# The z projection, its gate and norm inside the state-space units, and the late modulation inside the merge

## The reference, cut to what matters

```
y = y_ssd * silu(z)                                  # z = h @ w_z, 512 x 1024
yg = y in 4 groups of 256 columns
yg = yg * rsqrt(mean(yg * yg) + EPS)
ys = (yg * g_ssd_norm) @ w_branch_ssd
ya = o_attn @ w_branch_attn
mix = (sigmoid(g_a) * ya + sigmoid(g_s) * ys) @ w_out
```

## Time and profile before

| | us |
|---|---|
| median of 3 runs | 3477.12 (3476.56 to 3481.98) |
| the profiled execution | 3473.39 |
| its span | 3471.7 |
| PE busy in the span | 3009.3 (87%) |
| VectorE busy | 1838.7 (53%) |
| ScalarE busy | 1370.1 (39%) |
| GpSimd busy | 469.2 (14%) |
| mean granted clock | 0.933 |

### The profile page before, as it was taken

How to read it: one execution, slowest core, us unless ns; L and a number is a source line. 1 busy time by engine, 2 the same in 40 slices (tenths; PEclk the granted TensorE clock), 3 DMA queues, 4 the chain that set the end, 5 groups by cost and what they waited for, 6 DMA issues and landing times. The chain is left out here.

```text
span 3471.7 us, 37403 instructions
## 1 busy us (share of the span) xinstructions
PE 3009.3 (87%) x14782; PEld 2431.3 (70%) x14782; DVE 1838.7 (53%) x2198; ACT 1370.1 (39%) x1810; POOL 469.2 (14%) x524
## 2 busy tenths in 40 slices
PE   7976679798698679999999359979999897889998
PEld 4854568687487548777777248668888796668887
DVE  4456663535332448888888453644543415545543
ACT  3311222516222328788787122333332323433332
POOL 0006102212000052223222100000000004100000
PEclk9988889999799689999999779989999998999999
DMA  5200450200431339999998640043322202033321
GB/s 185 55 0 1 163 183 1 62 12 1 133 89 45 110 141 360 359 362 369 379 374 325 276 133 21 29 82 97 107 89 96 73 26 82 25 62 97 97 97 49
DMA packets 319998, 455.61 MB, mean 131 GB/s; under 512 B 69552, under 2 KB 251440, under 8 KB 298704
## 3 DMA queue, kind: packets, MB, share of 16 engines
q1 hardware_dynamic: 299136, 419.40, 35.4%
q0 software_dynamic: 20688, 33.82, 2.7%
HBM read 450.77 MB, written 39.08 MB: 141 GB/s over the span
## 5 line engine op out<-in xcount | busy, mean ns | idle before, releaser
L274 PE MATMUL banks<-hT_r,weight_part 128*128 128x512 f32 x1056 | 428.2, 405 | 72.9 <-DVE weight_part L234 58.4
L234 DVE TENSOR_TENSOR weight_part<-weights,weight_part 128x2048 fp32r<-128x2048 f32 (+1 forms) x118 | 264.3, 2240 | 417.6 <-ACT weight_part L223 417.6
L279 PE MATMUL banks<-hT_r,weight_part 128*128 128x512 f32 x1056 | 418.2, 396 | 0.0
L223 ACT ACTIVATE weight_part<-weights 128x2048 fp32r<-128x2048 f32 (+1 forms) x118 | 218.8, 1854 | 346.3 <-PE banks L274 279.2
L278 PE MATMUL banks<-h_low,weight_part 128*128 128x512 f32 x864 | 337.8, 391 | 0.0
L274 PEld LDWEIGHTS banks<-hT_r,weight_part 128*128 128x128 f32 x1056 | 201.8, 191 | 120.9 <-DVE weight_part L234 59.9
L279 PEld LDWEIGHTS banks<-hT_r,weight_part 128*128 128x128 f32 x1056 | 200.8, 190 | 47.9
L278 PEld LDWEIGHTS banks<-h_low,weight_part 128*128 128x128 f32 x864 | 163.8, 190 | 37.7 <-issue 2.4
L1136 ACT ACTIVATE up_room<-banks,conv_bias,taps 128x512 f32<-128x512 f32 x88 | 68.1, 777 | 297.4 <-PE banks L279 297.4
L1177 DVE SCALAR_TENSOR_TENSOR up_room<-banks,taps,up_room 128x511 f32<-128x511 f32 x88 | 65.8, 749 | 225.2 <-ACT up_room L1136 225.2
L854 POOL TENSOR_SCALAR branch_mean<-branch_mean 128x1 f32<-128x1 f32 x16 | 3.5, 221 | 1124.1 <-ACT up_room L848 762.4
(11 more groups left out here) (633 smaller groups left out, 7937.9 us busy)
## 6 DMA issues: line engine op xcount, KB each, us to landing
weights<-in_w_e_gate SPq DMA_DIRECT2D x44, 1024.0 KB, 15.8
weights<-in_w_e_up SPq DMA_DIRECT2D x44, 1024.0 KB, 18.2
hT<-in_w_e_down SPq DMA_DIRECT2D x44, 1024.0 KB, 18.8
weights<-in_w_up SPq DMA_DIRECT2D x88, 512.0 KB, 5.1
gate_up<-in_w_e_gate SPq DMA_DIRECT2D x22, 1024.0 KB, 15.6
gate_up<-in_w_e_up SPq DMA_DIRECT2D x22, 1024.0 KB, 18.5
down<-in_w_e_down SPq DMA_DIRECT2D x22, 1024.0 KB, 18.5
weights<-in_w_down SPq DMA_DIRECT2D x20, 1024.0 KB, 5.0
```

The costliest lines, as they stand in the source:

```text
L223: c.nc.scalar.activation(self.parts[n % 2][0][:, 0:z], self.raw[n % RAW_SLOTS][:, 0:z], ACT.Copy).then_inc(self.high_ready, 1)
L234: c.nc.vector.tensor_tensor(low[:, 0:z], self.raw[n % RAW_SLOTS][:, 0:z], high[:, 0:z].bitcast(F32), ALU.subtract).then_inc(self.low_ready, 1)
L274: ins = c.nc.tensor.matmul(out, lhs[0], rhs[0], start=start, stop=False)
L279: return c.nc.tensor.matmul(out, lhs[1], rhs[0], start=False, stop=stop)
```

## The change

The stage gate_y is gone; its two halves go to two places.

Into the units block: units run group by group. The z weights of a group are taken at its first tile; PE projects z of unit i behind the diagonal products of unit i-1, into the bank whose content the exponential has just read. ScalarE takes SiLU of z; VectorE multiplies behind the final add. ScalarE squares two units later, GpSimd takes the root three units later, VectorE scales four units later (norm). The buffers change: the spread, the exponential and the masked product share one triple buffer, spin; one of the two masked CB lies in a triangle that is not needed any more. VectorE's order in a unit is: mask CB, scale unit i-4, states, skip and adds, masked multiplies of unit i, final add of unit i-1, gate of unit i-1. The parts of the split weights lie in x, the gate rows and the context part of x_ssd; the first tile of z is loaded and converted in the states block.

Into the merge: 32 steps on VectorE, five in each column block behind the odd tile's conversion. GpSimd issues their 32 transfers of 512 KB, two buffers in x; x is loaded again at the end, also by GpSimd. Collects 0 and 1 are in pair 0 of blocks 2 and 4, collects 2 and 3 behind the last product.

```diff
@@ project_residual
+            dve.wait_ge(x_back, 16)
             for t in range(NT):
                 nc.vector.tensor_tensor(c.x[:, t], c.x[:, t], f[:, t], ALU.add)
@@ block1_mixer
-            gate_y(c, w_in, h, xt, yT, cond, ssd_gain)
+            plain_transpose(c, lambda tile: xt[:, NC + tile], NT, KD, lambda k, tile: yT[:, k, tile * P:(tile + 1) * P], lambda k: ssd_gain[:, k:k + 1],
+                            ahead=[[(KD, FT2, cols(w_in, c0 + n * FT2, FT2))] for c0 in (Q0, K0) for n in range(2)])
-        merge(c, w_in, h, yT, oT, [a[:].rearrange("p k n -> p (k n)") for a in hc])
+        merge(c, w_in, h, yT, oT, [a[:].rearrange("p k n -> p (k n)") for a in hc], cond)
@@ ssd, states block
+            x_parts, gate_parts, xt_parts = c.rounded(c.x), c.rounded(c.gate), c.over(xt, "xt_part", [P, PART], F32R)
+            lent = [x_parts[:].rearrange("p t d -> p (t d)")[:, i * PART:(i + 1) * PART] for i in range(2)]
+            more = [gate_parts[:].rearrange("p t d -> p (t d)"), xt_parts[:]]
+            c.split.kept = more + lent if c.split.highs % 2 else lent + more
+            @block.sync
+                c.split.ahead(sp, z_tiles(w_in))
+            @block.scalar
+                c.split.high_ahead(c, act)
             @block.vector
                 ...
+                c.split.low_ahead(c, dve)
@@ ssd, units block
-        units = [(tile, g) for tile in range(NT) for g in range(SSD_G)]
+        units = [(tile, g) for g in range(SSD_G) for tile in range(NT)]
+        @block.sync
+            c.split.load(sp, z_tiles(w_in))
         @block.gpsimd
+            def root(j):
+                at = slice(j, j + 1)
+                pool.wait_ge(squared, j + 1)
+                nc.gpsimd.tensor_scalar(rs[:, at], rs[:, at], EPS, None, ALU.add).then_inc(lifted, 1)
+                pool.wait_ge(lifted, j + 1)
+                nc.gpsimd.tensor_tensor(rs[:, at], rs[:, at], c.half[:, 0:1], ALU.pow).then_inc(rooted, 1)
             for i, (tile, g) in enumerate(units):
-                if i >= 2:
-                    pool.wait_ge(done, i - 1)
                 if i >= 3:
                     pool.wait_ge(diag, i - 2)
                 ...
+                if i >= 3:
+                    root(i - 3)
+            for j in range(U - 3, U):
+                root(j)
         @block.tensor
                     if i >= 2:
                         pe.wait_ge(ready, i - 1)
+                        pe.wait_ge(silud, i - 1)
                 ...
+                if i < U:
+                    if tile == 0:
+                        w = [a[:].rearrange("p (k n) -> p k n", n=GP) for a in c.split.take(pe)]
+                    pe.wait_ge(expd, i + 1)
+                    for k in range(KD):
+                        last = mm3(c, c.ps[:, 4 * (i % 2) + 1, 0:GP], [a[:, k, tok] for a in h], [a[:, k] for a in w], k == 0, k == KD - 1)
+                    last.then_inc(z_done, 1)
         @block.scalar
+            def square(j):
+                act.wait_ge(gated, j + 1)
+                if j:
+                    act.wait_ge(squared, j)
+                nc.scalar.activation(sq, rows_of(j), ACT.Square, scale=1.0 / 16, accum_out=rs[:, j:j + 1]).then_inc(squared, 1)
+            c.split.high(c, act)
             for i in range(U):
                 act.wait_ge(done, i + 1)
-                if i >= 2:
-                    act.wait_ge(diag, i - 1)
-                nc.scalar.activation(mt[:, i % 2].rearrange("p d h n -> p (d h n)"), c.ps[:, b + 1:b + 3].rearrange("p b n -> p (b n)"), ACT.Exp).then_inc(expd, 1)
+                nc.scalar.activation(spin[:, i % 3].rearrange("p d h n -> p (d h n)"), c.ps[:, b + 1:b + 3].rearrange("p b n -> p (b n)"), ACT.Exp).then_inc(expd, 1)
+                if i % NT == 0 and i + NT < U:
+                    c.split.high(c, act)
+                if i >= 2:
+                    square(i - 2)
+                act.wait_ge(z_done, i + 1)
+                nc.scalar.activation(sz[i % 2], c.ps[:, b + 1, 0:GP], ACT.Silu).then_inc(silud, 1)
+            square(U - 2)
+            square(U - 1)
         @block.vector
+            def norm(j):
+                dve.wait_ge(rooted, j + 1)
+                nc.vector.tensor_scalar(rows_of(j), rows_of(j), rs[:, j:j + 1], None, ALU.mult)
+            c.split.low(c, dve)
             for i in range(U + 1):
                 ...
+                if i >= 4:
+                    norm(i - 4)
                 ...
-                    dve.wait_ge(diag, j + 1)
-                    nc.vector.tensor_tensor(x_g, skip[:], c.ps[:, b, GP:2 * GP], ALU.add).then_inc(ready, 1)
                 if i < U:
                     dve.wait_ge(expd, i + 1)
                     ...
                     last.then_inc(mixed, 1)
+                if i:
+                    dve.wait_ge(diag, j + 1)
+                    nc.vector.tensor_tensor(rows_of(j), skip, c.ps[:, 4 * (j % 2), GP:2 * GP], ALU.add).then_inc(ready, 1)
+                    dve.wait_ge(ready, j + 1)
+                    dve.wait_ge(silud, j + 1)
+                    nc.vector.tensor_tensor(rows_of(j), rows_of(j), sz[j % 2], ALU.mult).then_inc(gated, 1)
+                if i % NT == 0 and i + NT < U:
+                    c.split.low(c, dve)
+            for j in range(U - 3, U):
+                norm(j)
@@ merge
+            acc, stage = [c.x[:, 0], c.x[:, 1]], [c.x[:, 2], c.x[:, 3]]
             @block.sync
-                sp.dma_start(c.x[:], t["x"][0].rearrange("(t p) d -> p t d", p=P)).then_inc(x_back, 16)
                 c.split.load(sp, merge_tiles(c))
                 c.split.ahead(sp, residual_tiles(t["w_out"][0], KD))
-                sp.wait_ge(x_back, 16)
+            @block.gpsimd
+                for i, kind in enumerate((2, 5)):
+                    nc.gpsimd.dma_start(c.gate[:, i], t["b_ada"][:, kind * D:(kind + 1) * D].to_broadcast([P, D])).then_inc(bias_in, 16)
+                for j in range(STEPS):
+                    if j >= 2:
+                        pool.wait_ge(stepped, j - 1)
+                    nc.gpsimd.dma_start(stage[j % 2], t["ada_late"][j // 2][:, j % 2]).then_inc(late_in[j % 2], 16)
+                pool.wait_ge(stepped, STEPS)
+                for i, name in enumerate(("g_post_mix", "g_post_ffn")):
+                    nc.gpsimd.dma_start(stage[i], t[name].to_broadcast([P, D])).then_inc(post_in, 16)
+                pool.wait_ge(finished, 5)
+                nc.gpsimd.dma_start(c.x[:], t["x"][0].rearrange("(t p) d -> p t d", p=P)).then_inc(x_back, 16)
             @block.tensor
+                        if i in (2, 4):
+                            if pair == 0:
+                                collect((i - 2) // 2, b0 + 2)
+                            else:
+                                pe.wait_ge(finished, i // 2)
                 ...
+                pe.wait_ge(left, KD - 1)
+                collect(2, 0)
+                collect(3, 2)
             @block.vector
                 c.split.low(c, dve)
+                n = 0
                 for i in range(KD):
-                    for _ in range(2 if i + 1 < KD else 1):
+                    c.split.low(c, dve)
+                    if i in (2, 4):
+                        finish((i - 2) // 2)
+                    if i == KD - 1:
+                        dve.wait_ge(post_in, 32)
+                        post(0)
+                        post(1)
+                    while n < min(5 * (i + 1), STEPS):
+                        step(n)
+                        n += 1
+                    if i + 1 < KD:
                         c.split.low(c, dve)
```

More of the change, by code:

```diff
@@ L90, in over @@
         self.uid += 1
-        return self.nc.alloc_sbuf_tensor_at(f"{name}_o_{self.uid}", shape, dt, offset=start + 4 * skip)
+        tensor = self.nc.alloc_sbuf_tensor_at(f"{name}_o_{self.uid}", shape, dt, offset=start + 4 * skip)
+        self.placed[id(tensor)] = (tensor, name, start + 4 * skip, shape)
+        return tensor
     def sem(self, name):
@@ L2194, in _ @@
                         nc.vector.tensor_tensor(new, new, psum, ALU.add).then_inc(kept, 1)
+                c.split.low_ahead(c, dve)
     with ExitStack() as s:
-        dtail = c.sb(s, "dt_a_masked", [P, 2, 2, HG, P])
+        spin = c.sb(s, "dt_a_masked", [P, 3, 2, HG, P])
         xd = c.sb(s, "x_dt", [P, 3, 2, GP])
-        mt = c.split.raw[0].rearrange("p (i d h n) -> p i d h n", i=2, d=2, h=HG)
-        cb = c.sb(s, "masked_CB", [P, 2, P])
+        cb_own = c.sb(s, "masked_CB", [P, P])
         off = c.sb(s, "from_states", [P, 2 * GP])
-        skip = c.sb(s, "skip", [P, GP])
+        rs = c.sb(s, "z_rstd", [P, SSD_G * NT])
+        lent = [bT[:, i, 0:CTX] for i in range(SSD_G)]
+        sz, sq, skip = lent[0:2], lent[2], lent[3]
+        cb = [cb_own[:].unsqueeze(1), tri[:, ONES:ONES + 1]]
+        c.split.buffers(c, s)
         spread = c.sem("so_spread")
@@ L2297, in _, with z_tiles @@
                     for d in range(2):
-                        last = nc.vector.tensor_tensor(mt[:, i % 2, d], mt[:, i % 2, d],
```

(44 more changed lines are left out.)

197 lines of the change are left out of this document (42 added, 155 removed).

## The result

The changed kernel takes 3423.31 us (median of 4 runs, 3412.62 to 3430.0) beside 3479.55 for the kernel before (4 runs, 3476.56 to 3482.04): a ratio of 0.9841, with a 95% interval of 0.9817 to 0.9865. The forecast was 3426, the range 3404 to 3450.

What follows compares the result with a forecast made beforehand. VectorE's loop was taken to bound the units and PE the merge. The terms 2.3 + 27.1 + 1.0 + 5 - 93.1 + 3.4 + 3.8, less 1 for the first unit, gave -51.5: 3426 us, range 3404 to 3450.

Steps and rivals of the forecast that it cites:

- the tail: From the last unit's masked CB to the transposes: 11.7 us instead of 104.8, a gain of 93.1.
- The unit loop: State-space units: VectorE's loop sets the pace, z is hidden; period 9.0 us, 15 periods 135.8 instead of 108.7, +27.1.
- Rival 1: Units: GpSimd's spread comes late enough for the masked multiplies to run alone; period 7.8, 3408 us; chance 0.12.
- The term for the clock: Units: two at PE's lower clock, each late by 1.5 us for first products and 1 for z, +5.
- The +1.0 for conversions: Units: gate multiply and a conversion fall in VectorE's wait for PE; three conversions stick out by 0.3 us each.
- The table loads: ScalarE in the units: 1.28 us before each exponential and SiLU, hidden under z and the rest of the period, 0.
- Rival 2: Unit loop longer by 1 us, through a late exponential or z in the loop: 16 us more, 3442; chance 0.14.
- The merge's steps: VectorE in the merge: 32 steps of at most 1.28 us, five per block in 15.6 us of room, no stall, 0.
- L: Merge: time from a step's end to its successor's landing, taken as 4.5 us; no stall while under 5.9.
- Rivals 3 and 4: Merge waits for steps: 3442 at 7 us per landing, 3476 at 9.4, chance 0.07; slower than before from 9.5, 0.03.
- The collects: PE in the middle of the merge: four fp32 128x512 collects, 0.86 us each where one follows another, +3.4.
- The merge's end: Behind the last product: two collects, small adds, GpSimd's issue of x; x lands before it is read, +3.8 us.

Runs made afterwards that it cites:

- e3_spread_later: Changed kernel, with GpSimd's spread for unit i waiting until VectorE's masked multiplies of unit i-2 are done: 3404.06 us, ratio 0.9797.
- e2_no_switch: Changed kernel, with ScalarE taking the exponential of z in place of SiLU, so one table serves the block: 3412.7 us, one run.
- e4_one_ahead: Changed kernel, with one transfer of a merge step in flight instead of two: 3488.99 us, one run.
- e1_x_by_sp: Changed kernel, with SyncE instead of GpSimd issuing the load of x at the merge's end: 3410.21 us, ratio 0.9823.
- e6_both: Changed kernel, with x loaded by SyncE and GpSimd's spread after the masked multiplies, together: 3392.35 us, ratio 0.9767.
- e7_low_in_units: As e6_both, with the first z tile converted at the units' start instead of the end of the states block: 3389.61 us, ratio 0.9746.

## Why the prediction was right, and where it was not

**The bound and the tail** were read rightly. The z stage went for 10.2 us instead of 11.7, 36 us of cover took the load and ScalarE's conversion. The first masked CB came 2.7 us later instead of 2.3, but not by the conversion alone: from the states' last add to GpSimd's start it is 2.2 us more (260.14 to 263.87, before 260.63 to 262.16), the first unit's products took 1.0 more, at the lower clock for longer (granted 0.53 instead of 0.65 while PE ran them), and the stage before was 0.5 ahead.

**The unit loop** was right in its mechanism and nearly in size. The period came out at 9.27 instead of 9.0: the scaling at 0.27 instead of 0.3, the multiplies at 2.87 instead of 2.5. The sum had a slip: 15 periods of the 9.01 that its terms give are 135.2, not 135.8, so the term is +26.5 and the forecast 0.6 us too high by its own working. Rival 1 was priced per unit at 7.8, measured at 7.63, and came true in three of 15 units, two of them by ScalarE's conversions, which the forecast hadn't followed. The term for the clock was 5 us for two units; the trace has one, at 2.9 more than its like. The first unit gained 1.9 instead of 1 (7.10 beside 9.0). The +1.0 for conversions had the wrong reason: by its own numbers the conversion fits (0.42 + 0.42 + 2.29 behind the add's start, in 0.56 + 3.08), and the trace agrees, 0.52 us of wait are left. What the two later conversions cost is 0.97 us each in the unit behind, by GpSimd's drawn-out spread. Together 27.5 instead of 32.1. e3_spread_later shows the contention at 18 us of that.

The Trainium skill (SBUF — State Buffer, Who interferes with whom) has this case: a VectorE instruction with two SBUF inputs contends with a GpSimd instruction that reads SBUF. The traces agree, 1.50 against 0.69, and the final add with one input in PSUM keeps its 0.41 in both.

**The table loads** at nothing: shown by e2_no_switch. The drain that the Trainium skill (ScalarE: Activation LUTs, What ACT_TABLE_LOAD costs) adds to each doesn't show in any row: each of the 31 loads starts within 0.03 us of the end of the instruction before it, and three times SiLU starts 0.02 us or less behind its load. Rival 2, built on a late exponential or on z in the loop, did not come: in every unit the exponential starts within 0.01 us of the masked CB.

**The merge's steps** at nothing: right to 0.1 us in this execution and to 1 us in the next, with nothing to spare, where the forecast's numbers left 2.7. L was taken as 4.5 us; in the tightest block it is 7.4 once and 4.3 once, 11.7 together, where 9.0 was forecast and 11.7 was the bound. With 3.76 for the steps beside them the chain is 15.4 of the 15.7 us that this block has (967.03 to 985.02, less the conversion's 2.28). The wait for a port that the forecast held possible didn't come, an issue took 0.53 to 0.56 us in all 32. Rivals 3 and 4 failed by their size only; e4_one_ahead shows their chain at 58 us between the first and the last block.

**The collects** cost +3.1 instead of +3.4 in the middle, two pairs at 1.72 less what varies elsewhere.

**The merge's end is the step that failed**: "now 4.0 + 0.5 for the small adds + 1.0 for GpSimd's issue of x". The parts named are there: the narrow records take 3.63, the adds are done by 1033.78, the issue takes 0.77. What was missing is that the block doesn't end with GpSimd's issue. It ends about when the 2 MB have landed, 8.4 us later. The forecast let x land "some 40 us before it is read", which is true of the reader and not of the block. With SyncE as the issuer the same edit costs 6.6 - 4.3 = 2.3 us instead of 12.0.

**What no part of the change touches**: the router's matmuls. These are the groups by line of the kernel before and of the changed one (busy, mean ns, idle before):

```profile
L3177 PE MATMUL banks<-weights,hT 128*128 128x64 f32 x64 | 13.5, 412 | 2.2 <-PEq L286 2.2
```

```profile
L3190 PE MATMUL banks<-weights,hT 128*128 128x64 f32 x64 | 7.3, 275 | 2.0 <-PEq L288 2.0
```

The same 64 instructions, at the lower clock in one profile and the higher in the other. The nine profiles fall in two groups: 7.3 us in the changed kernel, its repetition, e1_x_by_sp and e2_no_switch, 13.5 to 13.9 in the kernel before, e3_spread_later, e4_one_ahead, e6_both and e7_low_in_units. No kernel has been seen at both, so it isn't shown whether this is chance or belongs to the kernel. It is 6 of the 54 us, and why the profiled execution came out 2.6 below its forecast although the merge's end cost 8 more.

Left open: what makes one unit fall to the lower clock in one execution of the changed kernel and not in the other; what decides the clock of the router's matmuls; and whether GpSimd's block would end sooner with a smaller transfer, as it should if it waits for the landing.

## What to carry to other kernels

Ask of every transfer not only who reads it and when, but whose block it ends in: one issued late by GpSimd held the barrier for as long as the transfer took, one issued by SyncE did not. When two engines slow each other down, a wait that keeps them apart can be worth more than the overlap it forbids: one line gave 18 us here, because the slowed engine was on the loop and the delayed one was not. And when a stall is priced at nothing, write down its margin beside the zero: this one was 0.3 us in one profile and nothing in the next, and with one transfer in flight instead of two a gain of 56 us became a loss of 19.

## What the runs showed of the hardware

- The next block began 9.4 us behind the end of GpSimd's issue of a 2 MB load (8.4 us to landing), and 0.4 us behind the end of SyncE's issue of the same. In five profiles with GpSimd as the issuer it began 1.8 us behind the landing.
- GpSimd's issues of 512 KB took 0.53 us each, 32 times, with VectorE's two-input steps beside them or not (at most 0.56). They landed 3.9 to 8.0 us behind their issue, 4.6 at the median.
- ScalarE changed tables 31 times in 16 units, each load 1.28 us, and each went ahead of the wait of the activation behind it, where there was one.
- A scaling of one input by a column (128x256) took 0.35 us, but 1.00 at 308.19 of e3_spread_later, where GpSimd's spread was running.
